# Splitting two token quarters earlier and starting the first projection groups one row tile sooner, in a two-layer hybrid decoder kernel

## The reference, cut to what matters

```
def rms_norm(x, g):
    y = xf * lax.rsqrt(jnp.mean(xf * xf, axis=-1, keepdims=True) + RMS_EPS)
    return y * g
h = rms_norm(x, norm_pre[0])            # 1056 tokens x 1024
proj = h @ w_in[0]                      # 1024 x 4096
v, bg, cg, z = jnp.split(proj, 4, axis=-1)
u = cg * v
y = (bg * conv3(u) * silu(z)) @ w_out[0]
x = x + rms_norm(y, norm_post[0])
```

## Time and profile before

| | |
|---|---|
| median of 3 runs | 1118.16 us (1117.78 to 1118.46) |
| profiled execution, its own time | 1116.92 us |
| its span in the trace | 1115.2 us |
| TensorE busy | 1090.1 us, 98% of the span |
| VectorE busy | 734.4 us, 66% |
| ScalarE busy | 374.7 us, 34% |
| mean granted TensorE clock | 0.997 of full speed |

### The profile page before, as it was taken

One profiled execution on the slowest core, in us unless ns is written; L12 is line 12 of the kernel. 1 busy time (PEld: TensorE's weight loads), 2 busy tenths in 40 slices (PEclk: granted clock), 3 DMA queues, 4 the chain that ended last, 5 costly groups with the idle time before them and its releaser, 6 DMA issues.

```text
span 1115.2 us, 19773 instructions
## 1 busy us (share of the span) xinstructions
PE 1090.1 (98%) x7689; PEld 1030.7 (92%) x7689; DVE 734.4 (66%) x1301; ACT 374.7 (34%) x706; POOL 28.8 (3%) x36
## 2 busy tenths in 40 slices
PE   5999999999999999999999999999999999998998
PEld 4999999999999888899999999999999999987885
DVE  6799677767768366718476574866659476585246
ACT  7343333333335244521241321314222241432223
POOL 2000000000000000000000010100101001010000
PEclk8999999999999999999999999999999999999999
DMA  7002211211212532212121121111121120212043
GB/s 232 23 20 76 73 42 38 75 38 47 65 38 75 191 113 100 80 39 57 39 60 38 41 56 45 51 56 31 47 59 46 48 59 23 68 63 77 29 181 123
DMA packets 93315, 74.28 MB, mean 67 GB/s; under 512 B 2519, under 2 KB 85528, under 8 KB 93274
## 3 DMA queue, kind: packets, MB, share of 16 engines
q1 hardware_dynamic: 75482, 64.80, 18.6%
q10 hardware_dynamic: 17792, 8.91, 2.7%
HBM read 60.26 MB, written 13.44 MB: 66 GB/s over the span
## 4 chain that ended last, share of the span: by engine, by line
PE 96%; DVE 2%; ACT 0%; DMA 0%; issue 0%; SPq 0%; DVEq 0%; ACTq 0%
PE bank L547 33%; PE bank L587 26%; PE bank L686 16%; PE bank L567 4%; PE bank L759 4%; PE bank L754 1%; PE bank L807 1%; PE bank L789 1%; PE bank L839 1%; PE bank L832 1%; PE bank L841 1%; PE bank L701 1%; PE bank L667 1%; PE bank L663 1%; PE bank L827 1%; PE bank L767 1%
## 5 line engine op out<-in xcount | busy, mean ns | idle before, releaser
L547 PE MATMUL bank<-reg_a,wsplit 128*128 128x352 f32 x2304 | 389.9, 326 | 0.6 <-ACT arena L1195 0.6
L547 PEld LDWEIGHTS bank<-reg_a,wsplit 128*128 128x128 f32 x2304 | 368.3, 188 | 4.4 <-issue 2.3
L587 PE MATMUL bank<-reg_a,wsplit 128*128 128x264 f32 x1344 | 165.5, 284 | 0.0
L587 PEld LDWEIGHTS bank<-reg_a,wsplit 128*128 128x128 f32 x1344 | 164.1, 188 | 0.0
L587 PE MATMUL bank<-reg_b,w_ring 128*128 128x264 f32 x1008 | 124.8, 284 | 0.0
L587 PEld LDWEIGHTS bank<-reg_b,w_ring 128*128 128x128 f32 x1008 | 123.3, 188 | 0.1
L686 PE MATMUL bank<-reg_a,reg_b 128*128 128x512 f32 x288 | 69.9, 396 | 1.0 <-DVE reg_a L1377 1.0
L686 PE MATMUL bank<-reg_b,reg_a 128*128 128x512 f32 x288 | 68.7, 396 | 0.0
L686 PEld LDWEIGHTS bank<-reg_a,reg_b 128*128 128x128 f32 x288 | 53.8, 188 | 14.4 <-DVE reg_a L1377 1.7
L686 PEld LDWEIGHTS bank<-reg_b,reg_a 128*128 128x128 f32 x288 | 53.9, 188 | 12.6
L1760 DVE TENSOR_TENSOR arena<-arena,r_tt 128x512 f32<-128x512 f32 x40 | 27.6, 691 | 51.2 <-PE bank L759 47.6
(11 more groups left out here) (243 smaller groups left out, 1496.3 us busy)
## 6 DMA issues: line engine op xcount, KB each, us to landing
wraw<-in_w_in SPq DMA_DIRECT2D x64, 512.0 KB, 4.1
arena<-in_x_prompt SPq DMA_DIRECT2D x16, 512.0 KB, 3.8
wraw<-in_w_out SPq DMA_DIRECT2D x16, 512.0 KB, 3.3
x_scratch<-arena SPq DMA_DIRECT2D x8, 512.0 KB, 2.6
arena<-in_state_hgrn ACTq DMA_DIRECT2D x8, 512.0 KB, 3.9
out<-arena ACTq DMA_DIRECT2D x8, 512.0 KB, 2.9
arena<-x_scratch SPq DMA_DIRECT2D x8, 512.0 KB, 3.3
out<-arena SPq DMA_DIRECT2D x7, 512.0 KB, 2.6
```

Of the source, the lines that this page charges most:

```text
L547: mm = nc.tensor.matmul(bank[b][:, 0:CH], w[wi][:, k, :], rhs[hi], start=(k == 0 and i == 0), stop=(k == KT - 1 and i == 2))
L587: mm = nc.tensor.matmul(bank[banks[q]][:, 0:QT], w[wi][:, k, :], B_OP[name][hi][:, k, q * QT:(q + 1) * QT], start=(start and k == 0 and i ...
```

## The change

On TensorE each of the first groups moves ahead by one row tile: group 0 stands behind the turn of tile 3 rather than 4, and so on up to group 5 behind the turn of tile 8. Behind the turn of tile 2 stand 12 more transposes, of the identity into bank 0, and behind the turn of tile 3 eight more; nothing reads them. On ACT `token_hi(0)` and `token_hi(1)` stand ahead of `normalise(4)` and `normalise(6)` rather than behind them. On DVE `token_lo(0)` and `token_lo(1)` stand ahead of `normalise(4)` and the move of tile 3, and of `normalise(6)` and the move of tile 5, rather than behind these; `first_lo(1)` stands behind the move of tile 3 rather than 4. `token_hi(2)`, `token_hi(3)`, `token_lo(2)` and `token_lo(3)` stay where they are.

```
@@ TensorE
-            START = {4: 0, 5: 1, 6: 2, 7: 3, 8: 4}
+            def keep_busy(n):
+
+                for k in range(n):
+                    nc.tensor.transpose(bank[0][:, 0:P], ident[:, :], ident[:, :])
+
+            BETWEEN = {2: 12, 3: 8}
+            START = {3: 0, 4: 1, 5: 2, 6: 3, 7: 4, 8: 5}
             for i in range(TT):
                 turn_input(i)
+                if i in BETWEEN:
+                    keep_busy(BETWEEN[i])
                 if i in START:
                     first_group(START[i])
-            for g in range(5, 4 * NQ):
+            for g in range(6, 4 * NQ):
                 first_group(g)
@@ ScalarE
             for i in range(9):
+                if i in (2, 4):
+                    token_hi(i // 2 - 1)
                 if i + 2 < TT:
                     normalise(i + 2)
...
-                if i in (2, 4, 6, 8):
+                if i in (6, 8):
                     token_hi(i // 2 - 1)
@@ VectorE
                 r = P if i < 8 else NSAMP
+                if i in (3, 5):
+                    token_lo(i // 2 - 1)
                 if i < 8:
                     normalise(i + 1)
...
-                if i in (2, 4):
-                    first_lo(i // 2 - 1)
-                if i in (3, 5, 7):
-                    token_lo(i // 2 - 1)
+                if i in (2, 3):
+                    first_lo(i - 2)
+                if i == 7:
+                    token_lo(2)
```

## The result

The changed kernel takes 1127.88 us (median of 4, 1127.18 to 1130.19) against 1118.18 us before (median of 4). That is +9.7 us. The ratio on record is 1.0090, 95% interval 1.0078 to 1.0101; the two medians alone give 1.0087. Forecast were 1128.2 us and +10.0. The profiled execution took 1128.12 us, its span is 1126.4; it is 11.2 us longer than that of before, whose own time of 1116.92 us lay 1.3 us under its median.

What follows compares the result with a forecast made beforehand. TensorE, busy 98% of the span, was taken as the bound. -0.99 + 0.46 + 0.79 + 7.80 = +8.06, with the second clock fall +10.0: 1128.2 us median, range 1123.5 to 1130.5.

Steps and rivals of the forecast that it cites:

- What sets the time: Whole kernel: TensorE, busy 98% of the span, sets the time, so anything that delays it shows; no wait is for a transfer.
- What it loses, the kernel loses: Start of group 6, 44.1 us before: behind it work and distances stay the same, so its delay is the kernel's.
- Part 1: Start of group 0: token_hi(0) and token_lo(0) come sooner, so it begins at 20.19 us, -0.99 us.
- Part 2: Identity turns before group 0: they delay nothing; the clock falls again and group 0 takes 5.4 rather than 4.95 us, +0.46.
- Part 3: Between groups 0 and 1: the turn of tile 4 now stands on the path, +0.79 us; no wait for group 1.
- Part 4: Waits from the earlier order: 2.03 before group 2, 3.62 before 4, 0.84 before 5, 1.31 before 6; together 7.80 us.
- Part 5: Idle stretch of about 3.4 us before group 4: the clock falls again, +1.95 us, between 0 and 2.4.
- The sum: Whole kernel: +8.06 us without the second clock fall, +10.0 with it; median 1128.2 us.
- waits as forecast, clock falls once: Rival: the 3.4 us idle before group 4 are too short for a second clock fall; +8.1, 1126.2 us, chance 0.27.
- the case that was called the likeliest: All waits come and the clock falls twice, at groups 0 and 4: 1128.2 us, 1127 to 1129.5, chance 0.45.

Runs made afterwards that it cites:

- the identity turns only: Kernel before with 12 and 8 identity turns behind the turns of tiles 2 and 3, nothing else; 1118.76 us, ratio 1.0004.
- the second profile: Profile of the changed kernel itself, measured once more unchanged beside two other versions; median 1125.35 us, ratio 1.0066 against the kernel before.
- the profile with groups 4 and 5 back: Changed kernel with group 4 back behind the turn of tile 8 and group 5 behind it; 1124.43 us, ratio 1.0048 against the kernel before.
- filled version of before: Kernel before with 8, 19 and 23 identity turns behind the turns of tiles 2, 3 and 4; 1116.48 us, ratio 0.9980.
- the third split ahead: Changed kernel with DVE's token_lo(2) also ahead of the scaling of tile 8 and move of tile 7; 1124.77 us, ratio 1.0054 against before.
- the run with both long stretches filled: Changed kernel with 38 instead of 8 identity turns behind tile 3's turn and 32 behind tile 7's; 1125.96 us, ratio 1.0073 against before.
- the groups' order alone: Kernel before with only the groups one tile sooner on TensorE, splits unmoved, no identity turns; 1136.31 us, ratio 1.0149.

## Why the prediction was right, step by step

- **What sets the time.** Right: a delay of TensorE up to group 6 came out at the end undiminished. "What it loses, the kernel loses" was too simple on one side: 0.2 us crept in up to 102 us, and 1.5 us at 115, where the transfer of the next weights came late. That wait is in the changed kernel both times (1.5 and 1.4 us) and in four of the other profiles (1.6, 1.4, 0.6 and 0.5 us), but not in all that were delayed, and it is there (0.6 us) with the identity turns only, where nothing was delayed. So the likely cause is a transfer that lands with little to spare; before, ACT began the move that the product waits for at 104.67 us, a move takes 0.39, and the product began at 105.43. That is a margin of 0.4 us, and the transfer was waited for 1.9 us longer here. I had read from the trace of before that nothing waits for a transfer; the row showed no wait, but not how small the margin was.
- **Part 1**, -0.99: group 0 starts at 19.64, 1.54 us sooner. 0.56 of this is the load of tile 1, which landed earlier here (the move of tile 2 ends at 14.95 instead of 15.51). From there to group 0 it is 4.69 us against 5.67: -0.98. Right.
- **Part 2**, +0.46: group 0 took 4.19 us, -0.76, and 4.54 us in the second profile, -0.41. The sign was wrong: the clock did fall behind the identity turns, but at 21.2 us and not before the group. I had let it fall before the group and stay at half over all of it. The profile with groups 4 and 5 back shows that this can happen (5.35 us), so part 2 was one draw of several, and what the 20 turns did to it stays open. Transposes do count for the clock, as the rows of before had it and against the page of the Trainium skill named there (TensorE: Matmul & The Clock Gate, Part 4: PE-mode transpose). The filled version of before shows it, with the clock whole over 9 us of nothing but transposes.
- **Part 3**, +0.79: 1.16, because the turn of tile 4 fell in the half clock; 0.79 in the second profile. (20.19 + 3.00 + 0.79 is 24.0, not 23.9; nothing hangs on it.)
- **Part 4**, the core: 2.03, 3.62, 0.84 and 1.31 us forecast; 2.05, 3.61, 0.78 and 1.36 measured. The groups' order on TensorE makes them (they are there without the other parts of the change), and DVE's order sets the size of the one before group 4, which falls to 2.05 us with the third split ahead. In the changed kernel measured again they are the same.
- **Part 5**, +1.95: 1.4 us in the profile of one measurement and nothing in that of the other. Both lie in the bounds named, 0 to 2.4. As a fixed term of the sum it was wrong; it is a chance.
- **The sum.** To group 6: -1.54 - 0.76 + 1.16 + 2.05 + 3.61 + 1.44 + 0.78 + 1.36 = 8.1, forecast 10.0 with part 5. The 1.9 us less at this point (the parts on the clock and the earlier load) were made up behind it by 0.2 and 1.5 us, to 9.8. The last 1.3 us of the 11.2 between the two profiles, the cold stretch near the end, are as much as the profiled execution of before lay under its median, so the medians differ by 9.7. That the total met the +10.0 is partly luck; that the waits did is not.
- **The second measurement** says how much luck. It gives +7.8 us (ratio 1.0066), inside the range of 1123.5 to 1130.5, but it is the rival "waits as forecast, clock falls once" (+8.1) and not the case that was called the likeliest. Of its 8.4 us in the profile 6.95 are lost up to group 6: -1.3 for the start of group 0, -0.4 for its length, +0.8, the four waits of 2.04, 3.61, 0.80 and 1.35, and 0.1 for group 4. The forecast without part 5 was 8.06. The 1.4 us of the wait for the weights, which no part of the sum had, made up for the rest.

What stays open: why the clock falls more often behind the start with the identity turns alone (12 and 8), so that the median shows no gain, when 8, 19 and 23 leave 2.0 us; and whether the wait for weights at 115 us comes more often when the start is delayed.

## What to carry to other kernels

Before a consumer is moved ahead by one step in a fixed order, count the chain from its last input through every engine (here turn, move, high part, low part: 6.6 us) and compare it with what still lies between on the consumer's engine (here one group and two turns: 4.6 us). The order had been covering that chain, and nothing in the trace of before shows it as a wait. An idle stretch that ends in a cold clock can be filled with harmless turns for a small gain. Here the gain showed in the median only where all three stretches were filled, and it took many executions to see it.

## What the runs showed of the hardware

- The granted clock fell while TensorE was at work: at 21.2 us, 1.5 us into group 0, behind an idle stretch of 3.74 us, and in the run with both long stretches filled at 31.4 us, 1.3 us into group 2, behind one of 1.83 us. Both falls lasted 3.3 us, at the cost of the group then running. In six other profiles the same idle stretch of 1.8 us before group 2 was followed by no fall.
- The same 20 identity turns in the same place, with the same idle stretch of 3.7 us behind them, were followed by a fall at 21.2 us that lasted 3.3 us and by one at 18.6 us that lasted 6.8. Where the clock falls is not fixed by the order of the work alone.
- The same wait before group 4, 3.37 us idle, cost a fall in the first profile of the changed kernel and with the groups' order alone, and none in the second profile or without the identity turns. The medians of two sets of executions of one and the same kernel lie 2.5 us apart, and their intervals against the kernel before hardly overlap (1.0078 to 1.0101 and 1.0052 to 1.0080).
- Transposes keep the full clock: from 12 to 21 us of the filled version of before TensorE did nothing but turns of rows and of the identity, 8.65 us busy of 9, at 1.00.
